# A stick-breaking attention whose "one minus" moves from ScalarE to GpSimd

## The chip, the cores and the metric

The kernel runs on one core of a Trainium2 chip. The metric is the device time of one execution in microseconds (us); the time of a kernel is the median of several executions. TensorE (PE in the profile) multiplies matrices and writes PSUM, VectorE (DVE) and ScalarE (ACT) compute elementwise on SBUF and PSUM, GpSimd (POOL) computes on SBUF, and SyncE (SP) issues most of the transfers.

## The reference, cut to what matters

One decoder layer for 1024 prompt tokens and 8 sample tokens: a half FFN, a mixer of stick-breaking attention beside a state-space model, a cross-attention, another half FFN. The change touches only the prompt's stick-breaking attention, 8 heads of 64:

```python
def sb_weights(z, q_pos, k_pos):
    mask = k_pos[None, :] < q_pos[:, None]
    log_keep = jnp.where(mask, jax.nn.log_sigmoid(-z), 0.0)
    after = lax.cumsum(log_keep, axis=z.ndim - 1, reverse=True) - log_keep
    return jnp.where(mask, jnp.exp(jax.nn.log_sigmoid(z) + after), 0.0)

def sb_prompt(q, k, v, bias):
    ...
        z = jnp.einsum('bqhd,bkhd->bhqk', q_blk, k).astype(F32) * scale + bias_f
        w = sb_weights(z, q_p, k_pos)
        return jnp.einsum('bhqk,bkhd->bqhd', w.astype(v.dtype), v)
```

In products instead of logarithms: a key's weight is sigmoid(z) times the product of (1 - sigmoid(z)) over all keys between it and the query.

## The kernel before, in words

The program is a chain of phases, each a block in which every engine has its own instruction stream, with a barrier between blocks: samples ahead, first FFN, input projection, **attention**, state-space model, memory, mixing, cross-attention, output product, second FFN. The matrix products outside attention split each float32 operand into a high and a low part and multiply three times (L111 to L113).

The function `attention` works in 32 steps: 4 pairs of heads times 8 blocks of 128 queries. Step s of a pair has (s % 8 + 1) * 128 keys, cut into chunks of at most 512, so 48 chunks in all, and both heads of the pair go through each. For a chunk:

- TensorE (`scores`, L2343, L2347) writes the scores of both heads into PSUM banks; two pairs of banks alternate, and the next but one chunk's scores wait for `chance`, the count of finished sigmoids of z.
- ScalarE (`odds`) reads the scores from PSUM twice: L2270 makes `keep` = sigmoid(-z), which is one minus sigmoid(z), and L2275 makes `w` = sigmoid(z). Both lie in SBUF, in three slots (`SLOTS`) that steps use in turn.
- When the step's last chunk is there, VectorE runs for each head a scan (L2325), the running product of `keep` from the last key backwards, in place, and then for each head the product L2329 of `w` and the shifted `keep`, in place in `w`. Each has two inputs in SBUF; the scan is given the same reversed stretch twice.
- TensorE transposes `w` (`turn`, L2369), ScalarE copies the result out of PSUM (`take`, L2296), and TensorE multiplies by the values (`values`, L2382). For every pair, keys and values are transposed too (L2362, L2288), and stored by SyncE; finished outputs are copied by L2301.

The order of the work is written out by hand. TensorE in iteration i: per chunk `turn(i-2)`, then `scores(i+1)`; at the end `values(i-3)`. ScalarE in iteration i: per chunk `odds(i)`, then `take(i-2)`. VectorE: per step scan, scan, product, product. GpSimd only makes constants at the start of the block (L2247 to L2251).

Of the kernel before, what the change touches and what calls it, by code (L numbers as in the profile page):

```python
# [21 lines left out]
ACT = mybir.ActivationFunctionType  # L22
# [3 lines left out]
P = 128  # L26
EPS = 1e-6
KD = 8
NP = 1024
# [907 lines left out]
class Kernel:  # L937
# [1250 lines left out]
    def attention(self):  # L2188
        nc, a, o, ps = self.nc, self.a, self.o, self.ps
        self.cursor = self.after_qkvu  # L2190
        self.oT = self.at("oT", [P, 4, NT])
        PAIRS, BLOCKS, HALF = 4, 8, 512
        STEPS = PAIRS * BLOCKS
        SLOTS = 3
        EDGE = NP
        keep = self.place("at_keep", [P, SLOTS, 2, NP + 4], 0, ring=True)
        w = self.at("at_w", [P, SLOTS, 2, NP])
        wT = self.at("at_wT", [P, 2, 2, NP])
        ktm, vtm = (self.at(f"at_{n}", [P, 2, 8, P]) for n in ("k_rows", "v_rows"))
        bias = self.at("at_bias", [P, 8])  # L2200
        minus = self.at("at_minus", [P, 8])
        hide = self.place("at_hide", [P, P], 25, ring=True)
        later = self.place("at_later", [P, P], 26, dt=F32R, ring=True)
        one = self.place("at_one", [P, P], 27, dt=F32R, ring=True)
        MASKED = -1e30

        names = ("bias_in", "signed", "consts", "edges", "z_ps", "kept", "chance", "scanned", "weighted", "turned", "taken",
                 "k_rows", "v_rows", "pv", "out_sb")
        S = {n: self.sem(f"at_{n}") for n in names}
        stores = [self.sem(f"at_stores{r}") for r in range(2)]  # L2210
# [2 lines left out]
        def chunks(s):  # L2213
            n = (s % BLOCKS + 1) * P
            return [(n0, min(n, n0 + HALF)) for n0 in range(0, n, HALF)]

        first_chunk = [0]
# [15 lines left out]
        with nc.Block() as block:  # L2233
            @block.sync
            def _(sp):
                sp.dma_start(bias[:, :], a["sb_bias"].rearrange("(a n) -> a n", a=1).to_broadcast([P, 8])).then_inc(S["bias_in"], 16)
                sp.dma_start(self.z_dram, self.last.z[:, :]).then_inc(self.z_kept, 16)
                for j in range(PAIRS):
                    for name, rows, done in (("k_prompt", ktm, "k_rows"), ("v_prompt", vtm, "v_rows")):
                        sp.wait_ge(S[done], j * 2 + 2)  # L2240
                        sp.dma_start(o[name].rearrange("(b p) n -> p b n", p=P)[:, :, j * P:(j + 1) * P], rows[:, j % 2]).then_inc(stores[j % 2], 16)
                for r in range(2):
                    sp.wait_ge(stores[r], PAIRS * 16)

            @block.gpsimd
            def _(pool):
# [3 lines left out]
                                   pattern=[[-1, P]], channel_multiplier=1).then_inc(S["consts"], 1)  # L2250
                pool.memset(keep[:, :, :, EDGE:EDGE + 4], 1.0).then_inc(S["edges"], 1)  # L2251

            @block.scalar
            def _(act):
                act.wait_ge(S["consts"], 2)
                act.activation(later[:, :], hide[:, :], ACT.Copy).then_inc(S["consts"], 1)
                act.activation(one[:, :], self.ident[:, :], ACT.Copy).then_inc(S["consts"], 1)
                act.wait_ge(S["bias_in"], 16)
                act.activation(minus[:, :], bias[:, :], ACT.Copy, scale=-1.0).then_inc(S["signed"], 1)
                act.wait_ge(S["signed"], 1)  # L2260

                def odds(s, c):
                    j, t, off = s // BLOCKS, s % SLOTS, NP - chunks(s)[-1][1]
                    n0, n1 = chunks(s)[c]
                    m = first_chunk[s] + c
                    act.wait_ge(S["z_ps"], m + 1)
                    if s >= SLOTS:
                        act.wait_ge(S["weighted"], 2 * (s - SLOTS) + 2)
                    for h in range(2):
                        act.activation(keep[:, t, h, off + n0:off + n1], ps[2 * (m % 2) + h][:, 0:n1 - n0], ACT.Sigmoid,  # L2270
                                       bias=minus[:, 2 * j + h:2 * j + h + 1], scale=-0.125).then_inc(S["kept"], 1)
                    if s >= SLOTS:
                        act.wait_ge(S["turned"], number[of_step(s - SLOTS)[-1]] + 1)
                    for h in range(2):
                        act.activation(w[:, t, h, n0:n1], ps[2 * (m % 2) + h][:, 0:n1 - n0], ACT.Sigmoid,  # L2275
                                       bias=bias[:, 2 * j + h:2 * j + h + 1], scale=0.125).then_inc(S["chance"], 1)

                def take(item):
                    n = number[item]
                    act.wait_ge(S["turned"], n + 1)  # L2280
                    if item[0] == "rows":
                        _, j, which, half = item
                        if j >= 2:
                            act.wait_ge(stores[j % 2], j // 2 * 32)
                            if which:
                                act.wait_ge(S["pv"], (j - 1) * BLOCKS)
                        rows = (ktm, vtm)[which]
                        ins = act.activation(rows[:, j % 2, 4 * half:4 * half + 4],  # L2288
                                             ps[4 + n % 2].rearrange("p (b n) -> p b n", b=4), ACT.Copy)
                        ins.then_inc(S["v_rows" if which else "k_rows"], 1)  # L2290
                    else:
                        _, s, h, c = item
                        n0, n1 = chunks(s)[c]
                        if s >= 2:
                            act.wait_ge(S["pv"], s - 1)
                        act.activation(wT[:, s % 2, h, n0:n1], ps[4 + n % 2][:, 0:n1 - n0], ACT.Copy).then_inc(S["taken"], 1)  # L2296

                def out(s):
                    j, half = s // BLOCKS, s % BLOCKS // 4
                    act.wait_ge(S["pv"], s + 1)  # L2300
                    act.activation(self.oT[:, j, half * HALF:(half + 1) * HALF], ps[6 + half], ACT.Copy).then_inc(S["out_sb"], 1)  # L2301

                for i in range(STEPS + 4):
                    if i < STEPS and i % BLOCKS == 0:
                        for item in of_rows(i // BLOCKS):
                            take(item)
                    for c in range(2):
                        if i < STEPS and c < len(chunks(i)):
                            odds(i, c)
                        if 2 <= i < STEPS + 2 and c < len(chunks(i - 2)):  # L2310
                            for item in of_chunk(i - 2, c):
                                take(item)
                    if i >= 4 and (i - 4) % 4 == 3:
                        out(i - 4)
# [18 lines left out]
            def _(pe):  # L2333
# [17 lines left out]
                def turn(item):  # L2351
                    n = number[item]
                    if n >= 2:
                        before = items[n - 2]
                        if before[0] == "rows":
                            pe.wait_ge(S["v_rows" if before[2] else "k_rows"], before[1] * 2 + before[3] + 1)
                        else:
                            pe.wait_ge(S["taken"], sum(x[0] == "turn" for x in items[:n - 1]))
                    if item[0] == "rows":
                        _, j, which, half = item  # L2360
                        for b in range(4):
                            i = pe.transpose(ps[4 + n % 2][:, b * P:(b + 1) * P],  # L2362
                                             self.qkvu[:, (4, 8)[which] + j, (half * 4 + b) * P:(half * 4 + b + 1) * P], self.ident[:, :])
                    else:
                        _, s, h, c = item
                        n0, n1 = chunks(s)[c]
                        pe.wait_ge(S["weighted"], 2 * s + h + 1)
                        for b in range((n1 - n0) // P):
                            i = pe.transpose(ps[4 + n % 2][:, b * P:(b + 1) * P], w[:, s % SLOTS, h, n0 + b * P:n0 + (b + 1) * P],  # L2369
                                             self.ident[:, :])  # L2370
                    i.then_inc(S["turned"], 1)
# [858 lines left out]
```

## Time and profile before

| what | value |
|---|---|
| three timed runs | 2967.69, 2966.68, 2958.84 us, median 2966.68 |
| the profiled execution, its own time | 2960.39 us |
| its span, first to last instruction | 2958.7 us |
| mean granted TensorE clock | 0.952 of full speed |
| attention block, from its first instruction to the next block's first | 1309.7 to 1477.6 us |
| VectorE's part of it, first scan to end of last product | 1317.75 to 1470.65 us |

The profile gives, for one execution, the busy time of each engine, groups of instructions by source line with their mean durations, and who waited for whom. A duration in it runs from an instruction's start to its end, so whatever holds an instruction up after its start is part of it. A row of the windows view gives the stretch from start to end and its length, then for PE, PE's weight loads, DVE, ACT and POOL the busy time with the number of instructions, the granted TensorE clock, and the share and rate of the transfers; asked for one line's instructions it gives only their engine. "Idle before" is the time in which the engine had nothing running just before an instruction, with the instruction whose end released it.

### The profile page before, as it was taken

The numbers are of one execution on the slowest core, as the hardware profiler recorded it, in microseconds if no ns is written. First come the engines' busy times: TensorE is split into PE (matmuls) and PEld (weight loads), VectorE is DVE, ScalarE is ACT, GpSimd is POOL, SyncE is SP. The second block draws the span as 40 slices with busy tenths as digits, with TensorE's granted clock in tenths as the row PEclk, the third lists the DMA queues.
The fourth block names the chain that finished last, engine by engine and source line by source line (L and its number), as shares of the span: only waits on it lengthen the run. The fifth ranks groups of instructions, "written<-read, shape, count | busy, mean of one in ns | idle before, by whom it ended". The sixth has DMA issues, their size and how long they took to land. (4 is left out here: it accounts for less than half of the span.)

```text
span 2958.7 us, 44168 instructions
## 1 busy us (share of the span) xinstructions
PE 2719.3 (92%) x15387; PEld 2198.2 (74%) x15387; DVE 1842.5 (62%) x2530; ACT 802.7 (27%) x1461; POOL 349.5 (12%) x581
## 2 busy tenths in 40 slices
PE   6778899999999999998878889988989999999998
PEld 4456666666666677866534789873889999999998
DVE  6549999898898936768743372545254444444445
ACT  4221211212111124129822450422142111111115
POOL 1010032322222210210032000032000000000000
PEclk8779999999999999999978799999999999999999
DMA  9866698989989934531088431135111111111111
GB/s 356 310 231 198 187 338 311 330 298 308 314 303 306 318 116 145 170 92 30 15 290 274 144 121 46 43 118 181 54 32 52 50 43 50 43 50 43 43 55 60
DMA packets 334116, 478.19 MB, mean 162 GB/s; under 512 B 26600, under 2 KB 215397, under 8 KB 332110
## 3 DMA queue, kind: packets, MB, share of 16 engines
q1 hardware_dynamic: 291110, 333.29, 33.9%
q0 software_dynamic: 42416, 142.32, 14.2%
q8 instruction: 95, 1.56, 0.2%
q14 instruction: 87, 0.71, 0.1%
q10 hardware_dynamic: 408, 0.31, 0.0%
HBM read 453.22 MB, written 22.62 MB: 161 GB/s over the span
## 5 line engine op out<-in xcount | busy, mean ns | idle before, releaser
L84 ACT ACTIVATE whi<-raw 128x1024 fp32r<-128x1024 f32 (+1 forms) x184 | 189.2, 1041 | 747.4 <-PE banks L113 616.6
L111 PE MATMUL banks<-ffn_ghi,whi 128*128 128x344 f32 (+1 forms) x880 | 316.9, 360 | 34.3 <-DVE ffn_glo L1751 30.9
L111 PE MATMUL banks<-ffn_hhi,whi 128*128 128x344 f32 x1056 | 339.0, 321 | 7.4 <-DVE ffn_hlo L141 4.5
L112 PE MATMUL banks<-ffn_hlo,whi 128*128 128x344 f32 x1056 | 338.1, 320 | 0.0
L113 PE MATMUL banks<-ffn_hhi,wlo 128*128 128x344 f32 x1056 | 338.0, 320 | 0.0
L88 DVE TENSOR_TENSOR wlo<-raw,whi 128x1024 fp32r<-128x1024 f32 (+1 forms) x184 | 220.8, 1210 | 164.8 <-ACT whi L84 164.7
L113 PE MATMUL banks<-ffn_ghi,wlo 128*128 128x344 f32 (+1 forms) x880 | 312.1, 355 | 0.0
L112 PE MATMUL banks<-ffn_glo,whi 128*128 128x344 f32 (+1 forms) x880 | 311.3, 354 | 0.0
L111 PE MATMUL banks<-a_hhi,whi 128*128 128x512 f32 x704 | 287.9, 409 | 12.5 <-DVE wlo L88 12.5
L624 DVE TENSOR_TENSOR ffn_kt<-ffn_kt,ffn_q 128x1024 f32<-128x1024 f32 x224 | 272.5, 1216 | 31.8 <-DMA ffn_kt<-in_cache_k_dram 31.8
L611 POOL DMA_DIRECT2D ffn_vt<-in_cache_v_dram x384 | 206.1, 537 | 678.8 <-issue 676.3
L113 PE MATMUL banks<-a_hhi,wlo 128*128 128x512 f32 x704 | 278.5, 396 | 0.0
L112 PE MATMUL banks<-a_hlo,whi 128*128 128x512 f32 x704 | 278.3, 395 | 0.0
L629 DVE TENSOR_REDUCE ffn_z<-ffn_kt 128x16 f32<-128x1024 f32 x224 | 272.6, 1217 | 5.8
L111 PEld LDWEIGHTS banks<-ffn_ghi,whi 128*128 128x128 f32 x880 | 168.4, 191 | 74.9 <-issue 57.1
L111 PEld LDWEIGHTS banks<-ffn_hhi,whi 128*128 128x128 f32 x1056 | 199.7, 189 | 8.3 <-DVE wlo L88 4.8
L113 PEld LDWEIGHTS banks<-ffn_hhi,wlo 128*128 128x128 f32 x1056 | 199.4, 189 | 0.0
L112 PEld LDWEIGHTS banks<-ffn_hlo,whi 128*128 128x128 f32 x1056 | 199.1, 189 | 0.2
L111 PEld LDWEIGHTS banks<-a_hhi,whi 128*128 128x128 f32 x704 | 132.8, 189 | 88.1 <-issue 36.9
L2043 DVE SCALAR_TENSOR_TENSOR xT<-banks,xT 128x344 f32<-128x344 f32 x264 | 135.4, 516 | 98.1 <-PE banks L113 98.0
L113 PEld LDWEIGHTS banks<-ffn_ghi,wlo 128*128 128x128 f32 x880 | 167.8, 191 | 16.4
L112 PEld LDWEIGHTS banks<-ffn_glo,whi 128*128 128x128 f32 x880 | 168.5, 191 | 15.6 <-issue 1.0
(474 smaller groups left out, 4765.1 us busy)
## 6 DMA issues: line engine op xcount, KB each, us to landing
ffn_kt<-in_cache_k_dram SPq DMA_DIRECT2D x448, 256.0 KB, 4.3
ffn_vt<-in_cache_v_dram POOLq DMA_DIRECT2D x384, 256.0 KB, 4.8
raw<-in_w_ffn_gate_dram SPq DMA_DIRECT2D x44, 512.0 KB, 4.0
raw<-in_w_ffn_up_dram SPq DMA_DIRECT2D x44, 512.0 KB, 4.0
raw<-in_w_ffn_down_dram SPq DMA_DIRECT2D x44, 512.0 KB, 4.6
last_kt<-in_cache_k_dram POOLq DMA_DIRECT2D x64, 256.0 KB, 3.1
s_vt<-in_cache_v_dram POOLq DMA_DIRECT2D x64, 256.0 KB, 5.4
s_vt<-in_cache_v_dram SPq DMA_DIRECT2D x64, 256.0 KB, 4.9
```

What stands on the lines that cost most here:

```text
L84: act.activation(self.k.whi[c % W_RING][:, 0:self.width], self.slots[s][:, 0:self.width], ACT.Copy).then_inc(self.hi_done, 1)
L88: dve.tensor_tensor(self.k.wlo[c % W_RING][:, 0:self.width], self.slots[self.slot(n, c)][:, 0:self.width], self.k.whi[c % W_RING][:, 0:sel ...
L111: pe.matmul(out, whi, rhi, start=first, stop=False)
L112: pe.matmul(out, whi, rlo, start=False, stop=False)
L113: return pe.matmul(out, wlo, rhi, start=False, stop=last)
L611: pool.dma_start(self.vt[:, n % self.VR], self.values[:, ds(page, 1), :]).then_inc(self.v_in[n % self.VR], 16)
L624: v.tensor_tensor(keys, keys, q, ALU.mult).then_inc(self.k_times_q, 1)
L629: v.tensor_reduce(self.z[:, c * 16:(c + 1) * 16], self.kt[:, r].rearrange("p (h d) -> p h d", d=64), AX.X, ALU.add).then_inc(self.scored, 1)
L2043: v.scalar_tensor_tensor(out=x, in0=ps[DOWN[m]][:, 0:n], scalar=0.5, in1=x, op0=ALU.mult, op1=ALU.add).then_inc(added, 1)
```

## The change

L2270 and its operand `minus` go. ScalarE makes only `w` = sigmoid(z). GpSimd then computes `keep` = -1 * w + 1 from SBUF to SBUF, one instruction for each chunk and head, and counts `kept` itself; VectorE's scan still waits for `kept`. The wait of the `keep` slot for the products of three steps ago (`weighted`) moves with it from ScalarE to GpSimd.

```diff
-        minus = self.at("at_minus", [P, 8])
...
+                for s in range(STEPS):
+                    t, off = s % SLOTS, NP - chunks(s)[-1][1]
+                    if s >= SLOTS:
+                        pool.wait_ge(S["weighted"], 2 * (s - SLOTS) + 2)
+                    for c, (n0, n1) in enumerate(chunks(s)):
+                        m = first_chunk[s] + c
+                        for h in range(2):
+                            pool.wait_ge(S["chance"], 2 * m + h + 1)
+                            pool.tensor_scalar(keep[:, t, h, off + n0:off + n1], w[:, t, h, n0:n1], -1.0, 1.0, ALU.mult,
+                                               ALU.add).then_inc(S["kept"], 1)
...
-                act.activation(minus[:, :], bias[:, :], ACT.Copy, scale=-1.0).then_inc(S["signed"], 1)
-                act.wait_ge(S["signed"], 1)
...
                     act.wait_ge(S["z_ps"], m + 1)
-                    if s >= SLOTS:
-                        act.wait_ge(S["weighted"], 2 * (s - SLOTS) + 2)
-                    for h in range(2):
-                        act.activation(keep[:, t, h, off + n0:off + n1], ps[2 * (m % 2) + h][:, 0:n1 - n0], ACT.Sigmoid,
-                                       bias=minus[:, 2 * j + h:2 * j + h + 1], scale=-0.125).then_inc(S["kept"], 1)
                     if s >= SLOTS:
                         act.wait_ge(S["turned"], number[of_step(s - SLOTS)[-1]] + 1)
                     for h in range(2):
```

ScalarE in the steps of 512 to 768 keys of a pair, before (L2270 writes `at_keep`, L2275 `at_w`, L2296 takes the transposed weights):

```order
L2270 ACTIVATE at_keep<-banks,at_minus 128x512 x2
L2275 ACTIVATE at_w<-banks,at_bias 128x512 x2
L2296 ACTIVATE at_wT<-banks 128x384 x2
L2270 ACTIVATE at_keep<-banks,at_minus 128x128 x2
L2275 ACTIVATE at_w<-banks,at_bias 128x128 x2
L2270 ACTIVATE at_keep<-banks,at_minus 128x512 x2
L2275 ACTIVATE at_w<-banks,at_bias 128x512 x2
L2296 ACTIVATE at_wT<-banks 128x512 x2
```

and now (lines of the changed file; L2278 writes `at_w`, L2299 takes):

```order
L2278 ACTIVATE at_w<-banks,at_bias 128x512 x2
L2299 ACTIVATE at_wT<-banks 128x384 x2
L2278 ACTIVATE at_w<-banks,at_bias 128x128 x2
L2278 ACTIVATE at_w<-banks,at_bias 128x512 x2
L2299 ACTIVATE at_wT<-banks 128x512 x2
```

Every second sigmoid is gone; the rest keeps its order.

GpSimd from the start of the attention block, before:

```order
L2245 UNCONDITIONAL_BRANCH
L2247 MEMSET at_hide 128x128
L2249 AFFINE_SELECT at_hide<-at_hide 128x128
L2251 MEMSET at_keep 128x6x4
L2233 UNCONDITIONAL_BRANCH
```

and now, to the fourth step:

```order
L2244 UNCONDITIONAL_BRANCH
L2246 MEMSET at_hide 128x128
L2248 AFFINE_SELECT at_hide<-at_hide 128x128
L2250 MEMSET at_keep 128x6x4
L2260 ISA
L2260 TENSOR_SCALAR at_keep<-at_w 128x128 x2
L2260 TENSOR_SCALAR at_keep<-at_w 128x256 x2
L2260 TENSOR_SCALAR at_keep<-at_w 128x384 x2
```

Ninety-six TENSOR_SCALAR instructions stand on a queue that was empty in this block. One ISA instruction, which before stood ahead of the first TENSOR_TENSOR of cross-attention (L3030), now stands ahead of the first of them.

## Rows read from the trace of the kernel before

**Rows 1.** The page, section 1: busy time, share of the span, instructions
```profile
PE 2719.3 (92%) x15387; PEld 2198.2 (74%) x15387; DVE 1842.5 (62%) x2530; ACT 802.7 (27%) x1461; POOL 349.5 (12%) x581
```

**Rows 2.** Busy time by engine from first scan to last product (windows view)
```profile
1317.75:1470.65 152.90, 130.91 (x1084) 85.59 (x1084) 125.31 (x128) 138.79 (x303) 0.00 (x0) 0.98 0.09 25
```

**Rows 3.** The same for one pair of heads, the third
```profile
1392.20:1431.40 39.20, 34.16 (x298) 23.01 (x298) 31.36 (x33) 35.95 (x80) 0.00 (x0) 1.00 0.10 29
```

**Rows 4.** Who waited for whom, 1310 to 1480: us, times, longest
```profile
DVE at_keep L2325 <- ACT at_keep L2270: 36.5, 28, 8.9
PEld banks L2343 <- ACT at_w L2275: 27.3, 18, 2.3
```

**Rows 5.** VectorE's timeline in the third pair: start, us, instruction, idle before
```profile
1394.30 1.27 DVE L2325 TENSOR_TENSOR_SCAN at_keep<-at_keep 128x256 f32<-128x256 f32 x2 [0.92 <-ACT at_keep L2270]
1399.16 1.81 DVE L2325 TENSOR_TENSOR_SCAN at_keep<-at_keep 128x384 f32<-128x384 f32 x2 [2.94 <-ACT at_keep L2270]
1402.20 2.34 DVE L2325 TENSOR_TENSOR_SCAN at_keep<-at_keep 128x512 f32<-128x512 f32 x2 [0.32 <-ACT at_keep L2270]
1408.52 2.87 DVE L2325 TENSOR_TENSOR_SCAN at_keep<-at_keep 128x640 f32<-128x640 f32 x2 [2.78 <-ACT at_keep L2270]
...
1424.77 4.47 DVE L2325 TENSOR_TENSOR_SCAN at_keep<-at_keep 128x1024 f32<-128x1024 f32 x2 [0.35 <-ACT at_keep L2270]
```

**Rows 6.** ScalarE's instructions of L2270 alone, window of rows 2
```profile
1317.75:1470.65 152.90, 51.09 (x95) 0.98 0.09 25
```

**Rows 7.** Groups by shape, 1310 to 1480: busy us, mean ns, idle before
```profile
L2275 ACT ACTIVATE at_w<-banks,at_bias 128x512 f32<-128x512 f32 x48 | 31.5, 736 | 0.0
L2325 DVE TENSOR_TENSOR_SCAN at_keep<-at_keep 128x1024 f32<-128x1024 f32 x8 | 17.9, 2279 | 1.4 <-ACT at_keep L2270 1.4
```

**Rows 8.** VectorE's instructions of L2329 alone, window of rows 2
```profile
1317.75:1470.65 152.90, 44.89 (x64) 0.98 0.09 25
```

**Rows 9.** Groups by shape on GpSimd, whole span
```profile
L3030 POOL TENSOR_TENSOR c_cache<-c_cache,c_qb 128x2048 f32<-128x2048 f32 x8 | 37.0, 4644 | 28.7 <-DMA c_qb<-xq_scratch 28.7
L895 POOL TENSOR_SCALAR_AFFINE_SELECT s_vmask<-s_vmask 32x512 f32<-32x512 f32 x4 | 2.4, 606 | 0.3
L2249 POOL TENSOR_SCALAR_AFFINE_SELECT at_hide<-at_hide 128x128 f32<-128x128 f32 x1 | 0.3, 287 | 0.1
L590 POOL MEMSET ffn_mask<- 128x512 f32 x1 | 0.5, 528 | 0.0
L2247 POOL MEMSET at_hide<- 128x128 f32 x1 | 0.2, 204 | 15.2 <-POOLq L3185 15.2
```

**Rows 10.** VectorE's timeline in cross-attention, 1965 to 1983 and from 1989.5
```profile
1965.79 1.22 DVE L3083 TENSOR_TENSOR c_p<-c_p,c_sums 128x1024 f32<-128x1024 f32 x1
1974.51 3.31 DVE L3083 TENSOR_TENSOR c_p<-c_p,c_sums 128x1024 f32<-128x1024 f32 x1
1989.94 2.28 DVE L3078 TENSOR_REDUCE c_s<-c_cache 128x8 f32<-128x2048 f32 x1
1992.34 3.99 DVE L3083 TENSOR_TENSOR c_p<-c_p,c_sums 128x1024 f32<-128x1024 f32 x1
```

**Rows 11.** GpSimd's timeline of the same stretch
```profile
1967.75 8.98 POOL L3030 TENSOR_TENSOR c_cache<-c_cache,c_qb 128x2048 f32<-128x2048 f32 x2 [6.52 <-DMA c_qb<-xq_scratch]
1976.69 5.50 POOL L3030 TENSOR_TENSOR c_cache<-c_cache,c_qb 128x2048 f32<-128x2048 f32 x1
1990.72 4.53 POOL L3030 TENSOR_TENSOR c_cache<-c_cache,c_qb 128x2048 f32<-128x2048 f32 x1 [8.53 <-DMA c_qb<-xq_scratch]
```

**Rows 12.** GpSimd, then ScalarE's table load and VectorE's first scan, attention's start
```profile
1310.26 0.11 POOL L2251 MEMSET at_keep<- 128x24 f32 x1
1315.98 1.28 ACT L2270 ACT_TABLE_LOAD   x1
1317.75 0.74 DVE L2325 TENSOR_TENSOR_SCAN at_keep<-at_keep 128x128 f32<-128x128 f32 x2 [8.91 <-ACT at_keep L2270]
```

**Rows 13.** GpSimd queue's rows of L3030: duration ns min/median/max, first and last start
```profile
L3030 POOLq MODIFY_POOL_CONFIG  x2: 1/1/1, 1961.2 to 1961.2; - x2
```

More of the change, by code:

```diff
@@ L2205, in attention @@
         MASKED = -1e30
-        names = ("bias_in", "signed", "consts", "edges", "z_ps", "kept", "chance", "scanned", "weighted", "turned", "taken",
+        names = ("bias_in", "consts", "edges", "z_ps", "kept", "chance", "scanned", "weighted", "turned", "taken",
                  "k_rows", "v_rows", "pv", "out_sb")
@@ L2258, in _ @@
                 act.wait_ge(S["bias_in"], 16)
-                act.activation(minus[:, :], bias[:, :], ACT.Copy, scale=-1.0).then_inc(S["signed"], 1)
-                act.wait_ge(S["signed"], 1)
                 def odds(s, c):
-                    j, t, off = s // BLOCKS, s % SLOTS, NP - chunks(s)[-1][1]
+                    j, t = s // BLOCKS, s % SLOTS
                     n0, n1 = chunks(s)[c]
```

## The prediction

> **What bounds the kernel now.** The page's busy times come first [rows 1]: over the whole span TensorE leads with 92% and ScalarE stands at 27%, so a cheaper ScalarE is worth something only where a stage waits for it. I therefore looked at the stage alone, from VectorE's first scan to its last product [rows 2]: 152.90 us, of which ScalarE is busy 138.79, TensorE 130.91, VectorE 125.31 and GpSimd nothing. One pair of heads in the steady part [rows 3] takes 39.20 us: ScalarE 35.95, TensorE 34.16, VectorE 31.36. The list of waits [rows 4] says who holds whom: VectorE's scans wait 36.5 us for the sigmoid of L2270 (8.9 of it before the first scan, so 27.6 inside the stretch, and 125.31 + 27.6 is the 152.9), and the score matmuls wait 27.3 us for the sigmoid of L2275 to free their banks. Nothing there waits for VectorE. So the stage is bound by ScalarE, closely followed by the other two. VectorE's idle time sits mainly at two places of a pair, 2.94 us before the scan of 384 keys and 2.78 us before that of 640; with 0.92, 0.32 and 0.35 at others and two of 0.24 and 0.29 not listed it is 7.8 us [rows 5].
>
> **The change part by part.**
>
> *ScalarE loses L2270.* That is 51.09 us of busy time in the stretch (95 of the 96 instructions, the first stands ahead of it) [rows 6]. ScalarE would be left with 138.8 - 51.1 = 87.7 us in 152.9 and stops being the bound. What is next is VectorE with 125.3 us: even with no gap at all the stage can't be shorter than that, so at most 27.6 us is to be had. L2275 still takes 0.65 us for 512 columns (31.5 us over 48) [rows 7] and now frees the banks earlier. The copy that made `minus` (about 0.2 us) goes as well, and at the start it about pays for the first link below.
>
> *GpSimd gains 96 instructions*: 48 of 512 columns and 16 each of 384, 256 and 128, or 36864 columns. The trace has no such instruction, so it is bounded. The nearest is an affine select, also one input from SBUF and one output: 0.606 us for 512 columns and 0.287 for 128 [rows 9], between them 0.106 us per 128 columns, so 0.499 and 0.393 for 384 and 256. The sum is 48 * 0.606 + 16 * (0.499 + 0.393 + 0.287) = 29.1 + 18.9 = 48.0 us. Below lies a memset, which reads nothing: 0.528 and 0.204 us, by the same rule 25.3 + 15.0 = 40.3 us. Above lies the TENSOR_TENSOR of L3030 with two inputs: 4.53 us undisturbed for 2048 columns [rows 11], 2.21 ns a column, 81.5 us. I take 48.0, since the affine select has the same number of inputs. In the Trainium skill, GPSIMD Engine Reference, section "Elementwise — side-by-side cycle accounting", a tight loop is given 769 ns for 512 elements; at that rate, as an estimate from the page, 36864 columns would be 55 us and the sum below 7 us more. No run here shows that number.
>
> *A new link in the chain.* The scan waited for a sigmoid; now it waits for a sigmoid and then a GpSimd instruction of 0.3 to 0.6 us. The switch instruction that now stands ahead of the first one was done at 1961.2 us in the kernel before, and L3030 could start no later than 1967.75 after it, where it was released by a transfer [rows 11, 13]; so it costs at most 6.5 us. Here GpSimd is free at 1310.4, and the first `w` can't be there before the table load ends at 1317.3 [rows 12]: hidden. Behind GpSimd's waits nothing else is queued in this block; the slot wait for `weighted` of three steps ago was met before ScalarE reached it and is met here.
>
> *Do the two engines run beside each other?* This decides. Cross-attention is the one place in the trace where GpSimd computes from SBUF while VectorE works. VectorE's TENSOR_TENSOR L3083 with two SBUF inputs takes 1.22 us alone, but 3.31 us when it starts at 1974.51: it ends at 1977.82, 1.13 us after the GpSimd instruction that was running had ended (1967.75 + 8.98 = 1976.73). At 1992.34 it takes 3.99 us and ends 1.08 us after GpSimd's end at 1995.25 [rows 10, 11]. The other way round, the GpSimd instruction that begins at 1976.69, beside the delayed one, takes 5.50 us instead of 4.53. A reduction with one SBUF input, at 1989.94, runs beside GpSimd from 1990.72 on and takes its usual 2.28 us. So an instruction of VectorE with two SBUF inputs and one of GpSimd that reads SBUF exclude each other for their whole length, and whoever comes second waits. All of VectorE's work in attention is of that kind, products and scans. That is also the rule of the Trainium skill, SBUF — State Buffer, section "Who interferes with whom", which speaks against this change; the trace agrees, with 3.31 us in place of 1.22.
>
> *The sum.* If they exclude each other, the stage's length is VectorE's work plus GpSimd's plus the time in which neither can work. VectorE 125.3, GpSimd 48.0. Off goes what a waiting instruction has already done of its fixed part: 1.22 against 1.13 us above, about 0.1 us for a handover; for 96 of them at most 10, and I take 5, since not every one meets a waiting partner. On goes the idle time of both: of the 7.8 us of a pair much is filled by GpSimd itself, whose instructions now stand where VectorE waited, and ScalarE is early; I keep 2 us for a pair, at the scan of 384 keys, where TensorE has the 16 transposes of the step of 1024 keys in front, so 8 us (bounds 0 and 27.6). 125.3 + 48.0 - 5 + 8 = 176.3 us, against 152.9: **23.4 us longer**. TensorE's 34.16 us a pair [rows 3] is far below the 44 that a pair then takes, and so is ScalarE, so neither adds.
>
> **How it stands to the runs.** The profiled execution took 2960.39 us itself, so its sum is 2983.8. The four executions lie in two pairs, 2958.8 and 2960.4, 2966.7 and 2967.7, with a mean of 2963.4; the median of the three timed ones is 6.3 above the profiled. I put the sum on that mean and forecast 2986.8 us. A difference of 0.3%, 9 us, is about what a measurement of this kernel can tell from none.
>
> **The rivals.**
>
> *They do not exclude each other here (faster).* In the cross-attention rows GpSimd reads two tensors, here one; and its instructions are short. If a one-input GpSimd instruction left VectorE's second input alone, the stage would be VectorE's 125.3 us plus what is left of its idle time. With ScalarE relieved but the link longer by up to 0.6 us, I leave 3 of the 7.8 us of a pair: 4 * 4.8 = 19 us less, 2944. It decides at the first scan that runs its normal 2.28 us for 1024 keys [rows 7] with GpSimd busy inside it. For it speaks the free reduction in the rows; against it that GpSimd's read was exactly what stretched. 12 in 100.
>
> *Only the products exclude GpSimd (no change).* The scan names one stretch twice and may need one read. Then 44.9 us of products [rows 8] exclude GpSimd's 48, which fit beside 83 us of scans, but each of 64 products may wait up to one GpSimd instruction: between 0 and 64 * 0.3 = 19 us against the 19 saved. About 2944 to 2963, middle 2955. 10 in 100.
>
> *GpSimd is dearer than an affine select.* At the two-input rate, 81.5 us, the same sum gives 125.3 + 81.5 - 5 + 8 = 209.8, or 57 us longer: 3020. It is told by a TENSOR_SCALAR of 512 columns over 0.8 us when nothing of VectorE runs. 16 in 100 for anything from about 15 us above the forecast.
>
> *The change doesn't do what it says*: excluded, since the order shows the sigmoids gone.
>
> **How the numbers follow.** The forecast's case has 62 in 100; its own range is 125.3 + 48.0 - 10 + 0 = 163.3 to 125.3 + 48.0 + 27.6 = 200.9, so 10 to 48 us longer, mostly 2974 to 3000. The range has to hold 8 in 10 and reaches down over most of the products' rival to 2956 and up into the dear GpSimd to 3015; left out are the faster rival and the dearest prices, some 19 in 100. Slower by over 0.3%: 62 + 16, less 6 for the low end of the forecast's case, 72. Within: these 6 and 6 of the products' rival, 12. Faster: 12 and 4, 16.
>
> **What the changed profile would show.** Right: in the stage ScalarE busy 88 us and no longer waited for by the scans; GpSimd 96 instructions; VectorE's recorded time well above 125 us, scans and products with a spread of durations at equal shape; the sum of undisturbed VectorE and GpSimd time close to the stage's length; the stage some 176 us; everything outside attention unchanged. Wrong would be: durations of scans at equal shape all equal (no exclusion), a GpSimd instruction of 512 columns far from 0.6 us, idle time of both engines at the pair's start far above 2 us, or a lower granted TensorE clock in the stage, which is 1.00 in the steady pair now [rows 3].

## The result, and the profile after

| | before | changed |
|---|---|---|
| median of 7 runs each | 2961.0 us (2947.6 to 2967.7) | 2974.4 us (2968.7 to 2980.4) |
| ratio, 95% interval | | 1.0041 (1.0021 to 1.0061) |
| profiled execution, span | 2958.7 us | 2967.3 us |
| first scan to end of last product ("the stage" below) | 152.9 us | 161.6 us |

The change makes the kernel slower, by 13.4 us in the medians. The forecast was 2986.8 us, 23.4 above the mean of 2963.4 that it started from. The sign and the main mechanism came out, the size did not. The profiled executions differ by 8.6 us, and so do their stages (161.6 - 152.9 = 8.7); the other 4.7 us of the medians are not located by any profile, and when the changed kernel was timed again (below) its ratio was 1.0020 (1.0000 to 1.0039).

The windows view of the changed kernel, over the stage (columns as in [rows 2]):

```profile
1315.20:1476.70 161.50, 139.03 (x1084) 90.71 (x1082) 147.72 (x128) 95.92 (x206) 117.50 (x95) 0.93 0.08 22
```

Against [rows 2], ScalarE fell from 138.8 to 95.9 us, not to the forecast 88: in the kernel before, the records of L2270 overlap their neighbours', and without them the rest still covers 100.0 us. VectorE, which does exactly what it did, went from 125.3 to 147.7, and the granted clock in the stage from 0.98 to 0.93. Groups by shape, with mean ns (lines of the changed file: L2328 is the scan, L2332 the product, L2260 GpSimd's one minus):

```profile
L2260 POOL TENSOR_SCALAR at_keep<-at_w 128x512 f32<-128x512 f32 x48 | 70.7, 1491 | 16.8 <-ACT at_w L2278 16.8
L2328 DVE TENSOR_TENSOR_SCAN at_keep<-at_keep 128x1024 f32<-128x1024 f32 x8 | 19.3, 2453 | 0.0
L2332 DVE TENSOR_TENSOR at_w<-at_w,at_keep 128x512 f32<-128x512 f32 x8 | 6.8, 889 | 0.0
```

A scan of 1024 keys took 2279 ns before [rows 7]. The product of 512 keys took 675 ns, now 889. GpSimd's instruction of 512 columns is recorded at 1491 ns in the mean. How long it is when nothing disturbs it, and what a disturbance looks like, is seen in single instructions of the third pair (timeline view: start, us, instruction):

```profile
1403.51 0.61 POOL L2260 TENSOR_SCALAR at_keep<-at_w 128x512 f32<-128x512 f32 x1
1403.57 1.62 DVE L2328 TENSOR_TENSOR_SCAN at_keep<-at_keep 128x512 f32<-128x512 f32 x1 [0.51 <-POOL at_keep L2260]
...
1408.47 1.57 DVE L2328 TENSOR_TENSOR_SCAN at_keep<-at_keep 128x640 f32<-128x640 f32 x1 [0.19 <-POOL at_keep L2260]
1408.93 1.51 POOL L2260 TENSOR_SCALAR at_keep<-at_w 128x512 f32<-128x512 f32 x1 [0.23 <-ACT at_w L2278]
```

The first GpSimd instruction comes first and takes 0.61 us; the scan of 512 keys that starts 0.06 us after it takes 1.62 instead of 1.19 us. The second comes into a running scan: the scan ends at 1408.47 + 1.57 = 1410.04, GpSimd at 1408.93 + 1.51 = 1410.44, only 0.40 us later. So of the 0.61 us 0.21 had been done while it waited. This is no single case. Undisturbed, GpSimd's instruction takes 0.29, 0.51 and 0.62 us for 128, 384 and 512 columns here, and 0.40 for 256 in the run with halves below. Of the 96 records 76 are longer than that because VectorE was running, and each of them ends before its bare time has passed since VectorE's instruction ended: 0.13 to 0.21 us of it had been done, 12.7 us in all.

Who waits for whom has turned:

```profile
ACT at_wT L2299 <- PE banks L2372: 58.0, 46, 3.4
POOL at_keep L2260 <- ACT at_w L2278: 45.1, 18, 7.7
DVE at_keep L2328 <- POOL at_keep L2260: 23.4, 10, 9.6
PE banks L2372 <- DVE at_w L2332: 15.8, 17, 2.9
```

ScalarE now waits for TensorE's transposes, and those wait for VectorE's products: 15.8 us, where before it was 0.4. VectorE's own waits are down from 36.5 us [rows 4] to 23.4, of which 9.6 lie before the first scan.

Laying the records of VectorE and GpSimd over each other divides the stage without a rest:

| part of the stage, us | before | changed |
|---|---|---|
| VectorE's work undisturbed | 125.3 | 125.3 |
| its records longer than that | 0 | 22.5 |
| GpSimd at work, VectorE not | 0 | 5.2 |
| neither | 27.6 | 8.6 |
| sum | 152.9 | 161.6 |

GpSimd's 48 us cost 22.5 + 5.2 = 27.7 us. The 125.3 is taken over from the kernel before. In the memset run below, where VectorE has fewer pauses, its undisturbed records cover 123.9 us; with that as the first row the cost is 29.1 us, so these figures are good to about 1.5 us.

**TensorE's clock.** The pairs of heads don't take the same time. The scans that begin a pair start at 1315.18, 1353.03, 1395.23 and 1434.63. The second and third pair in the windows view:

```profile
1353.03:1395.23 42.20, 37.14 (x296) 25.00 (x296) 36.47 (x33) 25.26 (x55) 30.17 (x24) 0.92 0.09 26
1395.23:1434.63 39.40, 34.30 (x296) 22.91 (x296) 37.04 (x34) 25.23 (x55) 31.03 (x25) 1.00 0.10 28
```

The same instructions, but one pair is 2.80 us longer at a mean granted clock of 0.92. In steps of 2 us at the start of the second pair:

```profile
1350.00:1352.00 2.00, 0.08 (x1) 0.11 (x2) 2.00 (x3) 0.00 (x0) 2.00 (x2) 1.00 0.00 0
1352.00:1354.00 2.00, 1.29 (x8) 1.02 (x8) 2.00 (x5) 0.60 (x1) 0.04 (x1) 0.70 0.00 0
1354.00:1356.00 2.00, 2.00 (x7) 0.65 (x5) 1.99 (x5) 0.60 (x1) 0.00 (x0) 0.50 0.03 8
1356.00:1358.00 2.00, 2.00 (x10) 1.87 (x10) 0.00 (x0) 0.55 (x1) 0.00 (x0) 0.50 0.00 0
```

TensorE stands for 2 us waiting for the products of the step of 1024 keys, then the clock is granted at 0.50 (1.2 GHz) for some 7 us, and just there it is TensorE that everybody waits for: VectorE is at 0.00 from 1356 on. At the start of the third pair TensorE stands equally long and the clock stays at 1.00:

```profile
1392.00:1394.00 2.00, 0.00 (x0) 0.00 (x0) 2.00 (x3) 0.00 (x0) 2.00 (x2) 1.00 0.00 0
1394.00:1396.00 2.00, 1.17 (x8) 0.84 (x8) 2.00 (x3) 0.60 (x1) 1.57 (x2) 1.00 0.00 0
```

The 39.4 us of a pair at full clock are hardly more than the 39.2 of the kernel before [rows 3]. The fourth pair has the fall again, from 1434.7 on, and takes 42.1 us. That suggested that the loss is mostly the clock's, and the experiments had to part the two.

### The profile page after: what moved, and what is told of

Same layout as the page of the kernel before. It is cut to its first block and busy times, and to the rows that moved or that the text cites. A ratio compares the mean times of both kernels' runs of the same rounds, so it can differ in the third digit from the quotient of the medians.

```text
span 2967.3 us, 44196 instructions
## 1 busy us (share of the span) xinstructions
PE 2724.3 (92%) x15387; PEld 2201.9 (74%) x15387; DVE 1866.4 (63%) x2530; ACT 759.9 (26%) x1364; POOL 467.9 (16%) x677
```

## The experiments

Each was compared with the kernel before on the same chip. The stage's length and the busy times are from each one's profile.

### GpSimd writes but does not read

```diff
-  pool.tensor_scalar(keep[:, t, h, off + n0:off + n1], w[:, t, h, n0:n1], -1.0, 1.0, ALU.mult, ALU.add).then_inc(S["kept"], 1)
+  pool.memset(keep[:, t, h, off + n0:off + n1], 0.999).then_inc(S["kept"], 1)
```

> The changed kernel with each GpSimd TENSOR_SCALAR replaced by a memset of the same columns and the same waits: it writes keep but reads nothing, so keep is a constant and the attention weights are not computed. Stage = first scan to end of last product; 152.9 us before, 161.5 changed. Theory H (an instruction of GpSimd that reads SBUF and one of VectorE with two SBUF inputs exclude each other, with about 0.2 us of GpSimd's fixed start hidden): VectorE's durations go back to 2.28 and 1.21 us at 1024 keys, its busy time from 147.7 to 125 or 126 us, the stage to 139 to 145 us, kernel 8 to 14 us faster than before. Rival R1 (the longer link sigmoid, GpSimd, scan is what costs, not the exclusion): the memset is nearly as long (0.53 us for 512 columns), so the stage stays at 157 to 162 us.

The windows view over its stage, and then three of its groups by shape:

```profile
1312.32:1449.42 137.10, 129.97 (x1084) 85.81 (x1084) 123.93 (x128) 94.49 (x206) 39.74 (x95) 0.97 0.09 27
```

```profile
L2260 POOL MEMSET at_keep<- 128x512 f32 x48 | 25.1, 526 | 35.0 <-ACT at_w L2277 24.9 <-DVE at_w L2331 9.9
L2327 DVE TENSOR_TENSOR_SCAN at_keep<-at_keep 128x1024 f32<-128x1024 f32 x8 | 17.9, 2274 | 0.0
L2331 DVE TENSOR_TENSOR at_w<-at_w,at_keep 128x1024 f32<-128x1024 f32 x8 | 9.3, 1208 | 0.0
```

The link is there, 0.526 us for 512 columns, but scans and products are back at 2274 and 1208 ns, GpSimd's memsets at their bare length too, and the stage is 137.1 us, a little below what H expected. Ratio to before 0.9937 (0.9910 to 0.9964); this kernel leaves out the computation of keep. R1 is out: the longer link costs at most some 2 us, the distance to the 135.1 us of the last experiment, which has no such link. The Trainium skill, SBUF — State Buffer, section "Who interferes with whom", says that a VectorE instruction with two SBUF inputs contends with a GpSimd instruction that reads SBUF, not with one that only writes; this run agrees, for scans as well. The run is also the rival "they do not exclude each other": relieving ScalarE was worth 152.9 - 137.1 = 15.8 us, where the rival had 19.

### The same reads beside the kernel before

```diff
+  for s in range(STEPS):
+      for c, (n0, n1) in enumerate(chunks(s)):
+          m = first_chunk[s] + c
+          for h in range(2):
+              pool.wait_ge(S["chance"], 2 * m + h + 1)
+              if 2 * m + h >= 2:
+                  pool.wait_ge(S["spared"], 2 * m + h - 1)
+              pool.tensor_scalar(spare[:, h, 0:n1 - n0], self.qkvu[:, 0, 0:n1 - n0], -1.0, 1.0, ALU.mult, ALU.add).then_inc(S["spared"], 1)
```

> The kernel before, with both sigmoids on ScalarE, and 96 TENSOR_SCALAR of the changed kernel's shapes beside it on GpSimd that read an idle tensor and write a spare one; nobody waits for them. H: VectorE's instructions stretch as in the changed kernel (busy 125.3 to 143 to 149 us); part of it goes into VectorE's 27.6 us of idle time, the stage grows by 4 to 15 us over 152.9. R1: nothing waits for GpSimd, so VectorE busy 125 to 127 us and the stage 152 to 154 us.

The same two views of this kernel:

```profile
1329.21:1486.12 156.91, 131.57 (x1084) 85.57 (x1084) 147.44 (x128) 139.23 (x303) 126.31 (x96) 0.98 0.08 23
```

```profile
L2335 DVE TENSOR_TENSOR_SCAN at_keep<-at_keep 128x1024 f32<-128x1024 f32 x8 | 21.0, 2660 | 0.0
```

Nobody waits for these instructions, and yet VectorE's busy time rises to 147.4 us and a scan of 1024 keys to 2660 ns. The stage grows by 4.0 us, at the low end of H; the other 18 us went into VectorE's idle time, which fell from 27.6 to 9.5. R1, which expected 125 to 127 us of VectorE, is out from this side too. Ratio 1.0022 (0.9999 to 1.0044).

### Twice as many instructions, and half as many

```diff
+  mid = (n0 + n1) // 2
-  pool.tensor_scalar(keep[:, t, h, off + n0:off + n1], w[:, t, h, n0:n1], -1.0, 1.0, ALU.mult, ALU.add).then_inc(S["kept"], 1)
+  pool.tensor_scalar(keep[:, t, h, off + n0:off + mid], w[:, t, h, n0:mid], -1.0, 1.0, ALU.mult, ALU.add)
+  pool.tensor_scalar(keep[:, t, h, off + mid:off + n1], w[:, t, h, mid:n1], -1.0, 1.0, ALU.mult, ALU.add).then_inc(S["kept"], 1)
```

> The changed kernel with each TENSOR_SCALAR of GpSimd split into two of half the columns (192 instead of 96). H (only the reading part excludes VectorE, the fixed start is hidden under VectorE's instruction): VectorE busy 145 to 151 us, stage 159 to 165 us, kernel within 4 us of the changed one. Rival R2 (the whole instruction excludes VectorE, as the prediction's sum had it): 96 more fixed parts of 0.15 us, VectorE's busy time up by 10 to 14 us and the stage at 171 to 176 us.

```profile
1319.84:1490.89 171.05, 141.21 (x1080) 91.89 (x1076) 138.48 (x127) 96.08 (x204) 145.72 (x190) 0.91 0.07 20
```

Both expectations failed in part. The record of the last product falls outside this row; with it the stage is 173.3 us, as R2 had it, but VectorE's busy time did not rise by 10 to 14 us, it fell from 147.8 to 140.7; the kernel's ratio is 1.0058 (1.0030 to 1.0085). What grew is the time in which GpSimd works and VectorE stands, from 5.2 to 22.6 us. GpSimd was busy 145.7 us (waits for VectorE included) and had become the engine that is waited for. Only 97 of the 192 records were held by VectorE: the start of an instruction is hidden only while VectorE has something to do.

The other way, one instruction for both heads of a chunk:

```diff
-  for h in range(2):
-      pool.wait_ge(S["chance"], 2 * m + h + 1)
-      pool.tensor_scalar(keep[:, t, h, off + n0:off + n1], w[:, t, h, n0:n1], -1.0, 1.0, ALU.mult, ALU.add).then_inc(S["kept"], 1)
+  pool.wait_ge(S["chance"], 2 * m + 2)
+  pool.tensor_scalar(keep[:, t, :, off + n0:off + n1], w[:, t, :, n0:n1], -1.0, 1.0, ALU.mult, ALU.add).then_inc(S["kept"], 1)
...
-  v.wait_ge(S["kept"], 2 * m - 1 + h)
+  v.wait_ge(S["kept"], m)
```

> The changed kernel with one TENSOR_SCALAR of GpSimd for both heads of a chunk, 48 instead of 96, of up to 1024 columns. The changed kernel's 96 cost the stage 27.7 us (22.5 in VectorE's lengthened records, 5.2 in which GpSimd worked and VectorE stood) where undisturbed they last 48. If 0.21 us of each instruction is hidden whatever its size: 48 last about 40 us undisturbed, 10 are hidden, cost 30, stage 162 to 166 us. If it is a share of the columns that is hidden: cost 23, stage 155 to 159 us.

```profile
1320.24:1485.38 165.14, 142.94 (x1084) 93.08 (x1080) 146.32 (x128) 95.43 (x204) 63.49 (x47) 0.90 0.07 21
```

The stage took 165.1 us, within the first expectation, and the kernel's ratio is 1.0037 (1.0020 to 1.0053). Priced as above, the 48 cost 21.0 us in VectorE's records and 7.5 beside it, 28.5 in all; the time of neither engine was 11.3. With the prices of [rows 9] the bare work is 65, 48 and 39 us for 192, 96 and 48 instructions; the cost was 38.0, 27.7 and 28.5. So 27, 20 and 11 us were hidden, or 0.14, 0.21 and 0.22 us an instruction: a piece of each, not a share of its columns, and less of it where GpSimd is the one in arrears. Single records say the same: of the 24 instructions of 1024 columns, 1.05 us undisturbed, 20 were held, and they ended 0.84 to 0.91 us after VectorE's, so 0.14 to 0.21 us was done, as with 512 columns.

### TensorE kept busy

```diff
                     else:
                         _, s, h, c = item
                         n0, n1 = chunks(s)[c]
+                        for _ in range({(7, 0, 0): 14, (7, 1, 0): 4, (6, 0, 0): 4}.get((s % BLOCKS, h, c), 0)):
+                            pe.transpose(ps[4 + n % 2][:, 0:P], self.qkvu[:, 4, 0:P], self.ident[:, :])
                         pe.wait_ge(S["weighted"], 2 * s + h + 1)
```

> The changed kernel with TensorE kept busy before the longest waits: 14 + 4 + 4 extra transposes for each pair, written to the bank that the next real transposes overwrite, issued before the wait for the products of the last two steps. Theory C: part of the lengthening is TensorE's clock, granted at 0.50 for some 6 us at three of the pairs' starts in the changed kernel and 1.00 there in the kernel before; pairs with the fall took 42.2 and 42.1 us, the pair without 39.4. C expects the granted clock at 1.00 from 1340 us on, each pair 39 to 40 us, the stage 155 to 158 us, the kernel 2 to 6 us faster than the changed one. Rival (the fall of the clock only falls into time in which TensorE waits anyway): the stage stays at 160 to 163 us with the clock at 1.00.

```profile
1350.00:1352.00 2.00, 2.00 (x28) 1.83 (x30) 2.00 (x2) 1.30 (x4) 2.00 (x2) 1.00 0.45 131
1352.00:1354.00 2.00, 2.00 (x24) 1.72 (x18) 2.00 (x2) 0.30 (x1) 2.00 (x2) 1.00 0.00 0
1354.00:1356.00 2.00, 1.29 (x11) 0.92 (x10) 2.00 (x3) 0.60 (x1) 2.00 (x2) 1.00 0.00 0
1356.00:1358.00 2.00, 2.00 (x13) 1.29 (x14) 2.00 (x6) 0.60 (x1) 0.15 (x1) 1.00 0.00 0
```

The same stretch, with 22 useless transposes a pair (14 + 4 before the step of 1024 keys, 4 before that of 896): the clock stays at 1.00 at the starts of the second, third and fourth pair, the pairs take 39.4 us each (the scans of 128 keys start at 1317.91, 1355.80, 1395.17 and 1434.52), and the stage takes 155.7 us, 5.9 less than the changed kernel, with VectorE's busy time as long as there (148.3) and the time of neither down from 8.6 to 3.2 us. C holds for the stage. (The third fall that the expectation counts is at the start of the first pair; the kernel before has one there as well, from 1317.8 us. In the filled kernel the clock fell once more in the last step, at 1467.8 us.)

The times of whole kernels say less. The filled kernel stood at 0.9998 (0.9977 to 1.0018) of the kernel before. The changed, the filled and the difference kernel (below) were run once more side by side:

> The changed kernel again, side by side with the filled and the difference kernel on one chip, since they were timed in different calls so far. Theory C (the fall of TensorE's clock at the pairs' starts makes the loss): ratio to before 1.003 to 1.006, granted clock at 0.5 to 0.7 for some us at one or more pairs' starts. Rival (the difference between calls is the chip's): this and the filled kernel within 0.1% of each other.

> The filled kernel again. C: ratio to before 0.998 to 1.001, 0.3 to 0.6% below the changed kernel of the same call; granted clock 1.00 from the second pair on. Rival: within 0.1% of the changed kernel.

Measured: changed 2974.4 us, ratio 1.0020 (1.0000 to 1.0039); filled 2969.0 us, ratio 1.0008 (0.9988 to 1.0027). The medians are 5.4 us apart, which is the stage's difference, but the intervals overlap. The changed kernel's ratio is below the 1.003 that C expected, the filled one's is within its range, and their distance of 0.18% lies between C's and the rival's. The profile of the repeated changed kernel is clearer, since there only one of three boundaries fell:

```profile
1374.05:1413.47 39.42, 34.30 (x296) 22.91 (x296) 37.04 (x34) 25.27 (x55) 31.09 (x25) 1.00 0.10 28
1413.47:1455.71 42.24, 37.17 (x296) 25.04 (x296) 36.67 (x34) 25.30 (x55) 30.54 (x25) 0.92 0.09 26
```

Its stage took 158.5 us: with two falls 161.6, with one 158.5, with none 155.7, about 2.9 us each. The repeated kernel has no extra transposes, and its pair without a fall takes 39.4 us, as the filled kernel's pairs do: so it is the clock that made the difference, not the transposes themselves. How many an execution has changes from one to the next; three is the most that this stage's boundaries allow. The repeated filled kernel had none, with a stage of 155.7 us again. Outside the stage, executions of one kernel differ by more than all this: attention began at 1306.4 us in one profile of the changed kernel and at 1327.1 in the other.

### A part of the work to GpSimd

```diff
+  by_pool = lambda s, c: c == 0 and len(chunks(s)) == 2
...
-  for h in range(2):
+  for h in range(0 if by_pool(s, c) else 2):
       act.activation(keep[:, t, h, off + n0:off + n1], ps[2 * (m % 2) + h][:, 0:n1 - n0], ACT.Sigmoid,
```

(GpSimd has the loop of the change for these first chunks, with a count of its own, and VectorE waits for both counts.)

> Half way: the kernel before, but in the steps of over 512 keys GpSimd makes keep of the first chunk (32 TENSOR_SCALAR of 512 columns, none of them the last link before a scan), ScalarE the rest. By the price found so far (0.29 us of the stage for each GpSimd instruction): VectorE's busy time 125.3 + 9 = 134 us, ScalarE 139 - 21 = 118 us, the granted clock stays 1.00 at the pairs' starts; VectorE's idle time 10 to 14 us, stage 145 to 149 us, kernel 4 to 8 us faster than before. Rival (the idle time of the kernel before hangs on the last chunk's two sigmoids, which stay): stage 150 to 156 us, no change.

```profile
1329.89:1478.92 149.03, 129.43 (x1084) 85.06 (x1084) 132.76 (x128) 120.55 (x271) 40.77 (x32) 0.99 0.08 24
```

The stage came to 149.0 us, 3.9 less than before, at the edge of the first expectation; the kernel's ratio was 1.0000 (0.9979 to 1.0021), so of the expected 4 to 8 us nothing shows. VectorE's busy time rose by 7.5 us for 32 instructions.

### One sigmoid and no one minus

Since keep is 1 - w, w times the product of the later keeps is that product minus itself times keep: the difference of two neighbours in the scan's result. ScalarE makes only keep, and w needn't exist before the weights:

```diff
-  v.wait_ge(S["chance"], 2 * m - 1 + h)
...
-  v.tensor_tensor(w[:, t, h, 0:n], w[:, t, h, 0:n], keep[:, t, h, NP - n + 1:NP + 1], ALU.mult).then_inc(S["weighted"], 1)
+  if s >= SLOTS:
+      v.wait_ge(S["turned"], number[of_step(s - SLOTS)[-1]] + 1)
+  v.tensor_tensor(w[:, t, h, 0:n], keep[:, t, h, NP - n + 1:NP + 1], keep[:, t, h, NP - n:NP], ALU.subtract).then_inc(S["weighted"], 1)
```

GpSimd's loop and the sigmoid into w (L2275) go, L2270 stays, and the score banks are freed by `kept`.

> One sigmoid per score and no GpSimd work: ScalarE makes only keep = sigmoid(-z); since keep = 1 - w, the weight w times the product after it is the difference of two neighbours of the scan, so VectorE's second instruction is a subtract of shifted keep instead of a multiply. H: VectorE undisturbed 125.3 us, ScalarE about 88 us, VectorE the bound; stage 135 to 142 us, 11 to 18 us less than before, ratio to before 0.994 to 0.996. Rival (VectorE's idle time comes from TensorE's order of work and not from ScalarE): stage 148 to 153 us, ratio 0.998 to 1.000.

```profile
DVE at_keep L2320 <- ACT at_keep L2270: 20.2, 10, 8.7
PE banks L2339 <- ACT at_keep L2270: 3.7, 9, 1.1
```

Waits of that kernel: VectorE's fell from 36.5 us [rows 4] to 20.2, 8.7 of it before the first scan. The stage took 135.1 us, in both executions that were profiled, at a granted clock of 1.00; 123.6 of it is VectorE's work. Ratio to before 0.9946 (0.9923 to 0.9970), median 2947.4.

> The difference kernel again: 0.994 to 0.996 of before, 0.9% below the changed kernel, stage 134 to 137 us.

The second time it took 2947.9 us, 0.9943 (0.9919 to 0.9967), and 26.5 us or 0.9% below the changed kernel. It beats both: ScalarE loses the same work as in the change, and nothing is added anywhere. By the arithmetic, a difference of neighbours gives up some of the float32 digits of a small weight; how many was not measured here, and it is the price to look at before this is used elsewhere.

## Why the prediction was right or wrong

**What bounds the stage, and what ScalarE's relief is worth.** Right. ScalarE was the bound; with nothing in its place VectorE is, and the stage falls to 137.1 us (memset) or 135.1 (difference). The 19 us that the rival put on it were 15.8 and 17.8.

**The new link.** Right that it costs little: the memset run has it and takes at most 2 us more than the kernel without it. The switch instruction ran at 1307.0 us, long before the first input.

**Exclusion.** Right, and shown from both sides: with the change's reads VectorE's busy time is 147.8 to 148.6 us (changed and filled kernels, two profiles each), with writes of nearly the same length 123.9, with reads that nobody needs 147.4. "For their whole length" was too strong, as the sum shows. Scans are held as products are, so the rival "only the products" is out.

**GpSimd's price.** Right: the undisturbed instruction of 512 columns took 0.61 us against the 0.606 of the affine select; "GpSimd is dearer" is out.

**The sum.** This is where it failed: "about 0.1 us for a handover; for 96 of them at most 10, and I take 5". What did not have to be paid measured 20.3 us (48.0 - 27.7), 0.21 us an instruction on average. The step took what a waiting VectorE instruction has already done, and left out what a waiting GpSimd instruction has done: 0.13 to 0.21 us in each of 76 records, 12.7 us. With the measured bare durations (48.9 us) and the 123.9 us of VectorE, 19.8 us are hidden, and some 7 remain for VectorE's side and whatever else there is, so that half was nearly of the size taken. The rows on record had the missing half: in [rows 10, 11] VectorE's instruction ends at 1977.82 and GpSimd's, begun at 1976.69, at 1982.19, 4.37 us later where it needs 4.53. (They also give 1.09 us where the prediction reads 1.13, so 0.13 a handover, and 12 to 13 for 96.) With 20.3 in place of 5 and 8.6 in place of 8 the sum reads 125.3 + 48.0 - 20.3 + 8.6 = 161.6; it must, since 20.3 is what the stage leaves over, and the checks on it are the single records and the merged run. The forecast's own bounds (10 to 48 us longer) were too high for the same reason: the stage grew by 8.7, and by 2.8 where the clock held.

**"TensorE's 34.16 us a pair is far below the 44 that a pair then takes, ... so neither adds."** Wrong. It added through its clock: it stands for 2 us or more at the pair's start, and where the clock then falls, 2.8 us are lost. That was named among the things that would make the prediction wrong, but had no term in the sum. The 8 us for the time of neither engine came out at 8.6, at the place it was put, before the scan of 384 keys, but mostly by another cause: 3.2 are left when the clock holds, the rest is the clock. That the total agrees is luck.

**Put together.** From 152.9: relieving ScalarE takes off 15.8 (memset run); letting GpSimd read adds 18.6 (155.7 - 137.1, at full clock); the clock adds 5.9 in the profiled execution (0 to 9 as an estimate, 2.9 for each of three boundaries): 161.6. The two large terms nearly cancel, and of the 8.7 us that are left the clock, which had no term in the sum, makes up 5.9.

## What to carry to other kernels

Work moved from ScalarE to GpSimd is not free where VectorE's instructions have two inputs in SBUF: here 48 us of GpSimd's reads cost 27.7 us beside VectorE, and memsets of the same shapes, which read nothing, cost nothing that shows. Price the move by what both engines do together, and deduct what a waiting instruction has already done on either side, here 0.13 to 0.21 us for GpSimd's and about 0.1 for VectorE's. Look also at TensorE's idle stretches of some 2 us next to full-clock work, because there a slower neighbour can cost clock as well. Before moving an operation, ask whether it is needed: the one minus was already in the scan's result.

## What the runs showed of the hardware

- A GpSimd `tensor_scalar` held up by VectorE does 0.13 to 0.21 us of its bare time (0.62 us at 512 columns, 1.05 at 1024) while it waits, in 76 of 96 records of the changed kernel and 38 of 48 of the merged one; one of 512 columns ended 0.40 us after the scan that held it.
- A scan that names the same SBUF stretch for both inputs is held by GpSimd's reads (1.62 us in place of 1.19 at 512 keys), and not by its writes (2274 ns at 1024 keys beside memsets).
- TensorE's granted clock went from 1.00 to 0.50 for some 7 us after a stand of about 2 us at two of three boundaries between pairs and not at the third, in one and the same execution, and at one of three in another; with 22 extra transposes a pair it stayed at 1.00 at all of these boundaries in both profiled executions.
